# A hybrid decoder block: the third attention group's row maxima with rounded operands and 64-row matmuls, and the last gate evicted without its function

## The chip, the cores and the metric

The kernel runs on one core of a Trainium2 chip. The metric is device time in microseconds (us) of that core. Five engines work side by side: PE (TensorE, matmuls; PEld is its weight loading), DVE (VectorE), ACT (ScalarE), POOL (GpSimd) and SP (SyncE, which here issues nearly all DMAs, in program order, on one queue). Each engine executes its own program in order and waits on semaphores.

## The reference, cut to what matters

The block computes, for 1024 tokens of width 1024, an RMSNorm, one large projection (`z = h @ w_in`), an HGRN2 recurrence over 8 heads, dilated window attention over 3 groups of 8 heads (of 64 channels), a gated merge of both branches and an output projection. The parts that the change touches:

```
q_b = apply_rope(aqkv[:, :, 0], cos, sin);  k_b = apply_rope(aqkv[:, :, 1], cos, sin)
for g, (window, dilation) in enumerate(((128, 1), (512, 4), (2048, 16))):
    s = einsum(q, k) * E ** -0.5, masked;  m = max(s);  p = exp(s - m);  l = sum(p);  o = p @ v
wts = exp(ms - max over groups(ms));  den = sum(wts * l);  num = sum(wts * o)
o_b = num / den * silu(ag)
```

The maximum `m` is subtracted before the exponential and cancels in `num / den`, so it only has to be near the true maximum. In the third group (dilation 16) a sequence of 1024 tokens gives 16 residues of 64 tokens.

## The kernel before, in words

The projection's weights come in chunks of 128 columns (512 KB). Each chunk takes two slots of the program, one for each half of the tokens; in a slot PE runs 24 matmuls of 128x512 (`project`, L682 to L684: rounded high parts and low parts of both operands in three products) into one of two PSUM banks `z_ps[0]` and `z_ps[1]`, and ACT evicts that bank. PE may start the projection of slot s+2 once the bank of slot s is evicted.

First come 8 heads of the recurrence with 6 chunks each. Then come 4 pairs of attention heads with 10 chunks each, that is 20 slots a pair (pairs 0 to 3; pairs 1 and 2 are one hardware loop). After pair 3 comes a tail, in which the last pair's attention is mixed with the first branch products (`branch`, L912 to L914), and then the merge and the output projection.

In a pair, chunks 0 to 5 are q and k of groups 0, 1 and 2 in turn, chunks 6 to 8 the three v, chunk 9 the gate `ag`. For each of the six q and k chunks: ACT evicts it to `zz[0]` (q) or `zz[1]` (k); SP copies `zz` with its 32-row quarters exchanged to `z_swap` (four DMAs of 128 KB, L501); DVE multiplies with cosine and sine (L1638, L1639) and adds (L1643, for group 2 L1603). Groups 0 and 1 are split into rounded high and low parts (`q_two`, `q_sh`, `k_two`, `k_sh`). Group 2 is kept in full f32: DVE's two adds of 64 rows in slot 12 write q to `q_sh[2][0]` and `q_sh[2][1]`, two adds in slot 14 write k to `k_sh[2]`. In these tiles the other 64 rows are zero, but for one row, which holds 1 in `k_sh` and later minus the maximum in `q_sh` (`rows_to_queries`, L441), so that the second product subtracts it.

The row maxima (`maxima`, L797) are matmuls of 128x128 or 128x256 into `pa` (and sometimes `pc`), reduced by DVE (`row_max`, L1524). The eight steps of groups 0 and 1 run behind the projections of slots 8 to 15, two matmul groups each (one per head h); those of group 2 all run behind slot 16. DVE does a slot's reductions in the slot behind. In pairs 1 to 3 PE may write head h of a step only when the same head of the step before is reduced (`mx_taken`, `max_count(u - 1)`; in pair 0 it has `pc` too and waits for `max_count(u - 3)`).

SP's program sets the order of transfers: for each chunk c it first loads the weights of chunk c+2 (L431, when DVE has split chunk c, `w_lo_done`) and then, for c from 1 to 6, issues the four `z_swap` copies of chunk c-1. ACT's eviction of v of group 0 (slot 12, L1196) overwrites `zz[0]` and so waits for DVE's q sums.

In the tail, ACT takes the last exponentials, the high parts of the branch inputs (`branch_hi`, L1244) and of the weights (`branch_w_hi`, L1251), and the logarithm and exponential of the denominators (L1213 to L1216). DVE splits the weights (L1690), and PE's second branch product starts when `w_lo_done` says that they are there. The gate `ag` of a pair is evicted in slots 18 and 19 with ACT's Silu (L1020) to `s_ag`, which is `z_swap`.

Of the kernel before, what the change touches and what calls it, by code (L numbers as in the profile page):

```python
# [28 lines left out]
P = 128  # L29
D_MODEL = 1024  # L30
SEQ = 1024
KT = D_MODEL // P
HEADS = 8
# [4 lines left out]
PAIRS = 4  # L38
EDIM = 64
# [59 lines left out]
def build(nc, d, out):  # L99
# [6 lines left out]
    with ctx:  # L106
# [87 lines left out]
        def place_side(name, g, h):  # L194

            sides[name][g][h] = place(f"{name}{g}{h}", [P, SEQ], f32r if g < 2 else f32)
# [5 lines left out]
        zz = [place(f"zz{s}", [P, SEQ]) for s in range(2)]  # L202
# [12 lines left out]
        m_rows = place("m_rows", [2, GROUPS, SEQ])  # L215
        s_ag, o_b, v_t = z_swap, r_den, zz[0]
# [57 lines left out]
        padded, row_cleared = sem("padded"), sem("row_cleared")  # L274
# [45 lines left out]
        PADS = 19  # L320
# [47 lines left out]
        def _(sp):  # L368
# [64 lines left out]
            def rows_to_queries(i):  # L433

                for g in range(GROUPS):
# [3 lines left out]
                    for h in range(2):  # L439
                        dst = q_sh[g][h][EDIM * (1 - h):EDIM * (1 - h) + 1, :]  # L440
                        sp.dma_start(dst.bitcast(f32) if g < 2 else dst, m_rows[h:h + 1, g, :]).then_inc(rows_in[g], 16)  # L441

            def attention(i, prev, cur):
                for c in range(AT_CHUNKS):
# [42 lines left out]
                    if cur and 1 <= c <= 6:  # L487
# [11 lines left out]
                        for q in range(4):  # L499
                            o = q ^ 1  # L500
                            sp.dma_start(z_swap[32 * q:32 * q + 32, :], zz[(c - 1) % 2][32 * o:32 * o + 32, :]).then_inc(swapped, 16)  # L501
                    if first(i) and c == 4:
# [74 lines left out]
        def _(pool):  # L577
# [28 lines left out]
            def pad_group(g):  # L606

                for h in range(2):
                    other, row = slice(EDIM * (1 - h), EDIM * (2 - h)), slice(EDIM * (1 - h), EDIM * (1 - h) + 1)
                    as_f32 = lambda ap: ap.bitcast(f32) if g < 2 else ap  # L610
                    pad(as_f32(q_sh[g][h][other, :]), 0.0)
# [11 lines left out]

            for i in range(1, PAIRS):
                seen, cleared = value(pool, i * N_UNITS), value(pool, i * 2 - 1)
                pool.wait_ge(const_in, 32)
                pool.wait_ge(st_made, seen)
                nc.gpsimd.memset(q_sh[2][0][EDIM:EDIM + 1, :], 0.0).then_inc(row_cleared, 1)
                pool.wait_ge(row_cleared, cleared)
                nc.gpsimd.memset(q_sh[2][1][0:1, :], 0.0).then_inc(row_cleared, 1)  # L630
# [3 lines left out]
        def _(pe):  # L634
# [138 lines left out]
            def maxima(i, g, m, h):  # L773
# [5 lines left out]
                elif max_bank(i, g, m) is pc:  # L779
                    pe.wait_ge(ob_taken, i * N_SUMS)  # L780
# [4 lines left out]
                if g == 2:  # L785
                    pe.wait_ge(padded, PADS)
                    if not first(i):
                        pe.wait_ge(row_cleared, i * 2)
                    pe.wait_ge(rope_sum, i * 6 + 6)
                else:  # L790
                    pe.wait_ge(qk_lo_done, i * 4 + 2 * g + 2)
                    pe.wait_ge(q_dupped, i * 4 + 2 * g + h + 1)
                for blk, at, before in max_queries(g, m):
                    lo = blk - 1 if before else blk
                    at += 0 if before or g == 2 else P
                    q_side, k_side = (q_two[g][h], k_two[g][h]) if g < 2 else (q_sh[2][h], k_sh[2][h])
                    last = nc.tensor.matmul(max_bank(i, g, m)[:, h, at:at + P * (blk + 1 - lo)], q_side[:, P * blk:P * blk + P],  # L797
                                            k_side[:, P * lo:P * blk + P], start=True, stop=True)
                last.then_inc(mx_made, 1)

            def scores_t(i, u):
# [14 lines left out]
                pe.wait_ge(rope_sum, i * 6)  # L816
                units = unit_keys(g, m)
# [5 lines left out]
                for blk, at, n in units:  # L823
# [4 lines left out]
                    last = nc.tensor.matmul(dst, k_sh[g][h][:, ks], q_sh[g][h][:, qs], start=False, stop=blk == units[-1][0])  # L828
# [20 lines left out]
            def attention(i, prev, cur):  # L849
                for slot in range(2 * AT_CHUNKS):  # L850
# [25 lines left out]
                    if cur:  # L876
                        for g, m in MAX_SLOTS.get(slot, ()):
                            for h in range(2):
                                maxima(i, g, m, h)
# [96 lines left out]
        def _(act):  # L976
# [145 lines left out]
            def attention(i, prev, cur):  # L1122
                for slot in range(2 * AT_CHUNKS):
# [20 lines left out]
                    if cur and 4 <= slot <= 10 and hf == 0:  # L1144
# [6 lines left out]
                        for h in range(2):  # L1151
                            rows = slice(EDIM * h, EDIM * (h + 1))
                            nc.scalar.activation((q_two, k_two)[j % 2][j // 2][h][rows, :], zz[j % 2][rows, :], ACT.Copy).then_inc(qk_hi_done, 1)
# [659 lines left out]
```

## Time and profile before

| | us |
|---|---|
| median of 3 runs | 1509.67 |
| lowest, highest | 1508.07, 1510.61 |
| the profiled execution, its own time | 1508.62 |
| its span, first to last instruction | 1506.5 |
| PE busy | 1488.2 (99%) |
| PE weight loads busy | 1271.6 (84%) |
| DVE busy | 854.9 (57%) |
| ACT busy | 705.1 (47%) |
| granted TensorE clock, mean | 0.999 |

A busy PE is not PE at its peak: matmuls are pipelined, and a matmul's row is longer than its distance to the next one. So the cost of a matmul is read here from start to start.

### The profile page before, as it was taken

To read this page: it belongs to the slowest core of one execution; us is meant where nothing else is said; L and a number is where in the kernel's file an instruction comes from. 1 tells how busy PE (TensorE), PEld (TensorE's weight loads), DVE (VectorE), ACT (ScalarE), POOL (GpSimd) and SP (SyncE) were. 2 spreads that over 40 slices of the span, in tenths; PEclk is the share of its full clock that TensorE was granted. 3 is DMA by queue.
4 is the path that set the end of the run, shared out by engine and by line. 5 is a ranking of instruction groups with operands and counts; after the bars stand their busy time and mean duration, and the time that the engine had idled before them with its cause. 6 is when DMAs were issued, how large, how long until landed. Compare 5 with 4: busy or idle time off the path is not lost. (4 is left out here: it accounts for less than half of the span.)

```text
span 1506.5 us, 21102 instructions
## 1 busy us (share of the span) xinstructions
PE 1488.2 (99%) x7927; PEld 1271.6 (84%) x7927; DVE 854.9 (57%) x1387; ACT 705.1 (47%) x877; POOL 33.3 (2%) x39
## 2 busy tenths in 40 slices
PE   7999999999999999999999999999999999999998
PEld 5888888888888888888888888888888888888987
DVE  6646555473646374667952586358635865644523
ACT  6646565665647474745522434344334435411212
POOL 1000000000000000001400000000000000000000
PEclk9999999999999999999999999999999999999999
DMA  5121111121111211122313212321232134332702
GB/s 217 43 70 57 53 46 69 56 70 56 53 58 56 70 45 66 56 70 71 89 53 87 68 36 79 86 70 33 81 85 70 31 105 135 118 119 100 263 29 84
DMA packets 35520, 116.84 MB, mean 78 GB/s; under 512 B 6200, under 2 KB 6520, under 8 KB 35448
## 3 DMA queue, kind: packets, MB, share of 16 engines
q1 hardware_dynamic: 35456, 115.94, 24.1%
q8 instruction: 46, 0.75, 0.2%
q14 instruction: 18, 0.15, 0.0%
HBM read 83.21 MB, written 20.02 MB: 69 GB/s over the span
## 5 line engine op out<-in xcount | busy, mean ns | idle before, releaser
L682 PE MATMUL z_ps<-h_hi,w_hi 128*128 128x512 f32 x1392 | 551.3, 396 | 0.6 <-ACT zz L1172 0.6
L684 PE MATMUL z_ps<-h_hi,w_lo 128*128 128x512 f32 x1392 | 542.8, 390 | 0.0
L683 PE MATMUL z_ps<-h_lo,w_hi 128*128 128x512 f32 x1392 | 542.2, 390 | 0.0
L684 PEld LDWEIGHTS z_ps<-h_hi,w_lo 128*128 128x128 f32 x1392 | 261.3, 188 | 55.6
L682 PEld LDWEIGHTS z_ps<-h_hi,w_hi 128*128 128x128 f32 x1392 | 261.7, 188 | 52.1 <-issue 1.6
L683 PEld LDWEIGHTS z_ps<-h_lo,w_hi 128*128 128x128 f32 x1392 | 261.8, 188 | 50.4
L1322 DVE TENSOR_TENSOR w_lo<-w_stage,w_hi 128x1024 fp32r<-128x1024 f32 x89 | 109.4, 1230 | 225.7 <-ACT w_hi L1012 225.2
L1020 ACT ACT_TABLE_LOAD x61 | 78.3, 1283 | 77.7 <-PE z_ps L684 77.0
L1120 ACT ACTIVATE pt<-pb 128x512 f32<-128x512 f32 (+1 forms) x80 | 43.4, 543 | 119.5 <-PE pb L828 119.2
L1012 ACT ACTIVATE w_hi<-w_stage 128x1024 fp32r<-128x1024 f32 x89 | 93.8, 1054 | 0.3
L845 PE MATMUL pc<-pt,vb 128*128 128x128 f32 x560 | 77.6, 279 | 1.2 <-ACT pt L1120 1.2
L1379 DVE TENSOR_TENSOR q_lv<-qq,ee 128x512 f32<-128x512 f32 x48 | 33.2, 691 | 74.5 <-ACT ee L1043 74.5
L1043 ACT ACTIVATE ee<-dd 128x1024 f32<-128x1024 f32 x56 | 59.3, 1059 | 26.2 <-DVE dd L1364 25.8
L845 PEld LDWEIGHTS pc<-pt,vb 128*128 128x128 f32 x560 | 69.2, 192 | 1.7 <-ACT pt L1120 1.4
L1172 ACT ACTIVATE zz<-z_ps 128x512 f32<-128x512 f32 x48 | 28.5, 594 | 86.8 <-PE z_ps L684 60.4
L1196 ACT ACTIVATE zz<-z_ps 128x512 f32<-128x512 f32 x24 | 14.4, 598 | 113.9 <-PE pb L894 53.4
L1524 DVE CUSTOM_DVE_ANT_0 pa<-pa,mask_b 128x256 f32<-128x256 f32 (+1 forms) x144 | 48.2, 386 | 12.5 <-issue 7.3
L709 PEld LDWEIGHTS pb<-q_lv,k_lv 128*128 128x128 f32 x384 | 50.2, 191 | 3.7
L1409 DVE COPY_PREDICATED scores<-level_mask,pb 128x512 f32<-128x512 uint8 x48 | 48.3, 1007 | 4.5 <-PE pb L709 3.2
L709 PE MATMUL pb<-q_lv,k_lv 128*128 128x128 f32 x384 | 50.5, 274 | 0.0
L912 PE MATMUL z_ps<-h_hi,w_hi 128*128 128x512 f32 x128 | 50.4, 393 | 0.0
L913 PE MATMUL z_ps<-h_lo,w_hi 128*128 128x512 f32 x128 | 49.8, 389 | 0.0
(257 smaller groups left out, 2202.6 us busy)
## 6 DMA issues: line engine op xcount, KB each, us to landing
w_stage<-w_in SPq DMA_DIRECT2D x88, 512.0 KB, 3.4
z_swap<-zz SPq DMA_DIRECT2D x96, 128.0 KB, 2.3
gate_d<-gate SPq DMA_DIRECT2D x16, 512.0 KB, 4.3
x_in<-x SPq DMA_DIRECT2D x8, 512.0 KB, 7.6
o_a_d<-o_a SPq DMA_DIRECT2D x8, 512.0 KB, 4.7
w_stage<-w_a SPq DMA_DIRECT2D x8, 512.0 KB, 3.8
cos_t<-gate_d SPq DMA_DIRECT2D x8, 512.0 KB, 4.6
sin_t<-gate_d SPq DMA_DIRECT2D x8, 512.0 KB, 3.6
```

Of the source, the lines that this page charges most:

```text
L682: nc.tensor.matmul(z_ps[hf][:], w_hi[s][:, k, :], h_hi[:, k, t], start=k == 0, stop=False)
L683: nc.tensor.matmul(z_ps[hf][:], w_hi[s][:, k, :], h_lo[:, k, t], start=False, stop=False)
L684: last = nc.tensor.matmul(z_ps[hf][:], w_lo[s][:, k, :], h_hi[:, k, t], start=False, stop=k == KT - 1)
L709: last = nc.tensor.matmul(dst[:, P * a:P * a + P], k_side, q_side, start=True, stop=True)
L845: last = nc.tensor.matmul(pc[:, bank, P * ((blk + q) % 4):P * ((blk + q) % 4 + 1)], vb[:, g, blk, EDIM * h:EDIM * h + P], pt[u % 2][:, at ...
L912: nc.tensor.matmul(dst, w_hi[b][:, wk, :], src_hi[:, k, t], start=k == 0, stop=False)
L913: nc.tensor.matmul(dst, w_hi[b][:, wk, :], src_lo[:, k, t], start=False, stop=False)
L1012: nc.scalar.activation(w_hi[s][:], w_stage[s][:], ACT.Copy).then_inc(w_hi_done, 1)
L1020: nc.scalar.activation(dst[:, HALF * hf:HALF * (hf + 1)], z_ps[hf][:], func, **kw).then_inc(z_taken[hf], 1)
L1043: nc.scalar.activation(ee[u % 2][:], dd[u % 2][:], ACT.Exp).then_inc(e_done, 1)
L1322: nc.vector.tensor_tensor(w_lo[s][:], w_stage[s][:], w_hi[s][:].bitcast(f32), ALU.subtract).then_inc(w_lo_done, 1)
L1409: nc.vector.copy_predicated(dst, mask, src).then_inc(lvl_taken, 1)
```

## The change: what it does

Group 2 of every pair:

- In slot 12 DVE makes one add of 128 rows in place in `zz[0]` instead of two of 64 rows. SP copies the two halves by DMA (256 KB each) to `q_sh[2][0]` and `q_sh[2][1]`; it does so between the `z_swap` copies of chunk 4 and the weights of chunk 8 (semaphore `q2_copied`).
- ACT's eviction in slot 12, which overwrites `zz[0]`, waits for these copies. In slot 14 ACT rounds each half into the other tile's other 64 rows (two activations of 64x1024, `q2_rounded`).
- In slot 14 DVE makes a third add, which writes the rounded k of both heads to the new tile `k_hi2` (it lies where `zz[1]` lies).
- The maxima of group 2 are 16 matmuls of 64 contracted rows on rounded operands, the two heads in turn, each head in its own half of the array's rows and its own PSUM bank (`maxima_of_both`). Before they were 16 matmuls of 128 rows in f32, one head after the other.
- GpSimd's clearing of rows of `q_sh[2]` goes, since the DMA copies and the rounding rewrite them.

The last pair's gate is evicted with Copy in slots 18 and 19, and ACT applies Silu in place to the whole 128x1024 tile in the tail's slot 13, behind the high parts of weight chunk 1 of the branches and ahead of the denominators' logarithm.

```diff
                     if cur and 1 <= c <= 6:
...
+                        if c == 5:
...
+                            sp.wait_ge(rope_sum, summed)
+                            if prev:
+                                sp.wait_ge(st_made, scored)
+                            for h in range(2):
+                                rows = slice(EDIM * h, EDIM * (h + 1))
+                                sp.dma_start(q_sh[2][h][rows, :].bitcast(f32), zz[0][rows, :]).then_inc(q2_copied, 16)
...
+            def maxima_of_both(i, m):
+
+                pe.wait_ge(q2_rounded, i * 2 + 2)
+                pe.wait_ge(rope_sum, i * 6 + 6)
...
+                    pe.wait_ge(mx_taken, i * N_MAX + max_count(14 + 2 * m if first(i) else 16))
+                for blk, at, _ in max_queries(2, m):
+                    cols = slice(P * blk, P * blk + P)
+                    for h in range(2):
+                        rows = slice(EDIM * h, EDIM * (h + 1))
+                        last = nc.tensor.matmul(max_bank(i, 2, m)[:, h, at:at + P], q_sh[2][1 - h][rows, cols], k_hi2[rows, cols], start=True, stop=True)
+                        if blk == 4 * m + 3:
+                            last.then_inc(mx_made, 1)
...
+                    if cur and slot == 14:
+
+                        act.wait_ge(q2_copied, i * 32 + 32)
+                        for h in range(2):
+                            rows = slice(EDIM * h, EDIM * (h + 1))
+                            nc.scalar.activation(q_sh[2][1 - h][rows, :], q_sh[2][h][rows, :].bitcast(f32), ACT.Copy).then_inc(q2_rounded, 1)
...
                             if g == 0 and hf == 0:
-                                act.wait_ge(rope_sum, i * 6 + 5)
+                                act.wait_ge(q2_copied, i * 32 + 32)
...
-                            take(n, hf, s_ag, ACT.Silu)
+                            take(n, hf, s_ag, ACT.Copy if isinstance(i, int) and i == PAIRS - 1 else ACT.Silu)
...
+                    if not cur and slot == 13:
+                        for s in range(2):
+                            act.wait_ge(z_taken[s], N_IN)
+                        nc.scalar.activation(s_ag[:], s_ag[:], ACT.Silu)
...
+                    if cur and slot == 12:
+
+                        dve.wait_ge(rope_a, i * 6 + 5)
+                        dve.wait_ge(rope_b, i * 6 + 5)
+                        nc.vector.tensor_tensor(zz[0][:], zz[0][:], z_swap[:], ALU.add).then_inc(rope_sum, 1)
+                    if cur and slot == 14:
...
                         for h in range(2):
                             rows = slice(EDIM * h, EDIM * (h + 1))
-                            dst = (q_sh, k_sh)[j % 2][2][h]
-                            last = nc.vector.tensor_tensor(dst[rows, :], zz[j % 2][rows, :], z_swap[rows, :], ALU.add)
-                        last.then_inc(rope_sum, 1)
+                            last = nc.vector.tensor_tensor(k_sh[2][h][rows, :], zz[1][rows, :], z_swap[rows, :], ALU.add)
+                        last.then_inc(k2_summed, 1)
+                        dve.wait_ge(k2_summed, i + 1)
+                        nc.vector.tensor_tensor(k_hi2[:], zz[1][:], z_swap[:], ALU.add).then_inc(rope_sum, 1)
```

SP's program in the loop of pairs 1 and 2, from the `z_swap` copies of chunk 4 on (`zz_125` is `zz[0]`, `zz_126` is `zz[1]`, `w_stage_52` takes the weights of chunk 8 and `w_stage_53` those of chunk 9). Before:

```order
L501 DMA z_swap<-zz_125 32x1024 x3
L431 ISA [waits w_lo_done,const_in]
L431 DMA w_stage_52<-w_in 128x1024
L301 REGISTER_ALU
L501 DMA z_swap<-zz_126 32x1024 [waits z_taken1,rope_sum,z_taken0,const_in]
L501 DMA z_swap<-zz_126 32x1024 x3
L431 ISA [waits w_lo_done,const_in]
L431 DMA w_stage_53<-w_in 128x1024
```

And now:

```order
L507 DMA z_swap<-zz_125 32x1024 x3
L305 ISA
L521 DMA q_sh_135<-zz_125 64x1024 [waits st_made,rope_sum,const_in]
L521 DMA q_sh_136<-zz_125 64x1024
L435 ISA [waits w_lo_done,const_in]
L435 DMA w_stage_52<-w_in 128x1024
L507 DMA z_swap<-zz_126 32x1024 [waits z_taken1,rope_sum,z_taken0,const_in]
L507 DMA z_swap<-zz_126 32x1024 x3
L435 ISA [waits w_lo_done,const_in]
L435 DMA w_stage_53<-w_in 128x1024
```

Both the q copies and the `z_swap` copies of chunk 5 wait for the same DVE sum (`rope_sum`, slot 12). Before, the weights of chunk 8 were issued ahead of that wait and the swap came first behind it; now two q copies and the weights stand between the sum and the swap.

ACT's program in the tail, from the last exponentials to the weights of the second branch product (`w_hi_54`). Before:

```order
L1120 ACTIVATE pt_131<-pb 128x512
L1244 ACTIVATE ob_hi<-sin_t 128x1024
L1244 ACTIVATE ob_hi<-zz_125 128x1024
L1251 ACTIVATE w_hi_55<-w_stage_53 128x512
L1213 ACT_TABLE_LOAD
L1213 ACTIVATE r_den<-acc_132 64x1024
L1214 ACTIVATE r_den<-acc_133 64x1024
L1216 ACT_TABLE_LOAD
L1216 ACTIVATE r_den<-r_den 128x1024
L1251 ACTIVATE w_hi_54<-w_stage_52 128x1024
```

And now:

```order
L1145 ACTIVATE pt_131<-pb 128x512
L1279 ACTIVATE ob_hi<-sin_t 128x1024
L1279 ACTIVATE ob_hi<-zz_125 128x1024
L1286 ACTIVATE w_hi_55<-w_stage_53 128x512
L1245 ACT_TABLE_LOAD
L1245 ACTIVATE z_swap<-z_swap 128x1024
L1248 ACT_TABLE_LOAD
L1248 ACTIVATE r_den<-acc_132 64x1024
L1249 ACTIVATE r_den<-acc_133 64x1024
L1251 ACT_TABLE_LOAD
L1251 ACTIVATE r_den<-r_den 128x1024
L1286 ACTIVATE w_hi_54<-w_stage_52 128x1024
```

A table load and the Silu of 128x1024 now stand ahead of the logarithms and of `w_hi_54`.

## Rows read from the trace of the kernel before

**Rows 1.** The page, busy time of each engine, share of the span and instructions

```profile
PE 1488.2 (99%) x7927; PEld 1271.6 (84%) x7927; DVE 854.9 (57%) x1387; ACT 705.1 (47%) x877; POOL 33.3 (2%) x39
```

**Rows 2.** Timeline, PE, pair 1 slot 16: start us, us, operation, count, idle before

```profile
923.79 1.95 PE L797 MATMUL pa<-k_sh,q_sh 128*128 128x128 f32 x16
925.57 1.95 PE L797 MATMUL pc<-k_sh,q_sh 128*128 128x128 f32 x16
927.36 1.04 PE L894 MATMUL pb<-ident,zz 128*128 128x128 f32 x8
```

**Rows 3.** Timeline, weight loads of rounded operands, one unit of scores in the tail

```profile
1263.68 0.19 PEld L828 LDWEIGHTS pb<-q_sh,k_sh 128*128 128x128 f32 x1
1263.80 0.19 PEld L827 LDWEIGHTS pb<-q_two,k_two 128*128 128x128 f32 x1
```

**Rows 4.** Timeline, DVE, pair 1, slots 12 to 14

```profile
898.86 2.47 DVE L1603 TENSOR_TENSOR q_sh<-zz,z_swap 64x1024 f32<-64x1024 f32 x2
...
905.60 1.98 DVE L1638 TENSOR_TENSOR zz<-zz,cos_t 128x1024 f32<-128x1024 f32 x1 [1.73 <-DMA z_swap<-zz]
...
910.66 0.43 DVE L1524 CUSTOM_DVE_ANT_0 pa<-pa,mask_b 128x256 f32<-128x256 f32 x1
...
911.01 2.45 DVE L1603 TENSOR_TENSOR k_sh<-zz,z_swap 64x1024 f32<-64x1024 f32 x2
913.49 1.23 DVE L1322 TENSOR_TENSOR w_lo<-w_stage,w_hi 128x1024 fp32r<-128x1024 f32 x1
```

**Rows 5.** Timeline, SP's DMA issues, the same stretch

```profile
901.41 2.41 SPq L501 DMA_DIRECT2D z_swap<-zz  x4
904.07 0.38 SPq L431 DMA_DIRECT2D w_stage<-w_in  x1
```

**Rows 6.** The page, DMA issues: count, KB each, median us from issue to landing

```profile
w_stage<-w_in SPq DMA_DIRECT2D x88, 512.0 KB, 3.4
z_swap<-zz SPq DMA_DIRECT2D x96, 128.0 KB, 2.3
```

**Rows 7.** Timeline, PE, pair 1: starts of slot 14, its maxima, slot 16's start

```profile
905.34 0.39 PE L682 MATMUL z_ps<-h_hi,w_hi 128*128 128x512 f32 x1
...
910.79 0.92 PE L797 MATMUL pa<-k_two,q_two 128*128 128x128 f32 x4
...
918.34 0.39 PE L682 MATMUL z_ps<-h_hi,w_hi 128*128 128x512 f32 x1
```

**Rows 8.** Timeline, ACT, pair 1: evictions of slots 12 and 14

```profile
901.36 0.60 ACT L1196 ACTIVATE zz<-z_ps 128x512 f32<-128x512 f32 x1 [8.19 <-DVE q_sh L1603]
...
912.62 0.60 ACT L1196 ACTIVATE zz<-z_ps 128x512 f32<-128x512 f32 x1 [5.99 <-PE pb L894]
```

**Rows 9.** Timeline, ACT, the start of the tail

```profile
1248.04 0.60 ACT L1020 ACTIVATE z_swap<-z_ps 128x512 f32<-128x512 f32 x1 [3.42 <-PE z_ps L684]
1248.66 1.28 ACT L1120 ACT_TABLE_LOAD   x1
1249.95 0.60 ACT L1120 ACTIVATE pt<-pb 128x512 f32<-128x512 f32 x1
```

**Rows 10.** Timeline, PE, the same place

```profile
1249.13 0.28 PE L828 MATMUL pb<-q_sh,k_sh 128*128 128x256 f32 x1
1250.60 1.16 PE L845 MATMUL pc<-pt,vb 128*128 128x128 f32 x8 [1.19 <-ACT pt L1120]
```

**Rows 11.** Timeline, the tail's slot 13: ACT

```profile
1286.72 1.28 ACT L1213 ACT_TABLE_LOAD   x1
...
1292.44 1.04 ACT L1251 ACTIVATE w_hi<-w_stage 128x1024 fp32r<-128x1024 f32 x1
```

**Rows 12.** Timeline, DVE and then PE, behind it

```profile
1293.54 1.22 DVE L1690 TENSOR_TENSOR w_lo<-w_stage,w_hi 128x1024 fp32r<-128x1024 f32 x1
...
1294.81 0.19 PEld L912 LDWEIGHTS z_ps<-h_hi,w_hi 128*128 128x128 f32 x1 [0.20 <-DVE w_lo L1690]
1294.88 0.44 PE L912 MATMUL z_ps<-h_hi,w_hi 128*128 128x512 f32 x1
```

More of the change, by code:

```diff
@@ L201, in build @@
             place_side(name, g, h)
-        zz = [place(f"zz{s}", [P, SEQ]) for s in range(2)]
+        zz = [place("zz0", [P, SEQ])]
+        zz1_at = top[0]
+        zz.append(place("zz1", [P, SEQ]))
         z_swap = place("z_swap", [P, SEQ])
@@ L622, in _ @@
             assert pads[0] == PADS
[L624 to L630, printed above, removed]
         @block.tensor
@@ L784, in maxima @@
                     pe.wait_ge(mx_taken, i * N_MAX)
[L785 to L792, printed above, removed]
+                pe.wait_ge(qk_lo_done, i * 4 + 2 * g + 2)
+                pe.wait_ge(q_dupped, i * 4 + 2 * g + h + 1)
                 for blk, at, before in max_queries(g, m):
                     lo = blk - 1 if before else blk
[L795 to L798, printed above, removed]
+                    at += 0 if before else P
+                    last = nc.tensor.matmul(max_bank(i, g, m)[:, h, at:at + P * (blk + 1 - lo)], q_two[g][h][:, P * blk:P * blk + P],
+                                            k_two[g][h][:, P * lo:P * blk + P], start=True, stop=True)
                 last.then_inc(mx_made, 1)
+            def maxima_of_both(i, m):
+                pe.wait_ge(q2_rounded, i * 2 + 2)
+                pe.wait_ge(rope_sum, i * 6 + 6)
+                if max_bank(i, 2, m) is pc and not first(i):
+                    pe.wait_ge(ob_taken, i * N_SUMS)
+                else:
+                    pe.wait_ge(mx_taken, i * N_MAX + max_count(14 + 2 * m if first(i) else 16))
[6 more added lines that the diff above has]
+                            last.then_inc(mx_made, 1)
             def scores_t(i, u):
@@ L827, in scores_t @@
                         nc.tensor.matmul(dst, k_two[g][h][:, ks], q_two[g][h][:, qs], start=False, stop=False)
-                    last = nc.tensor.matmul(dst, k_sh[g][h][:, ks], q_sh[g][h][:, qs], start=False, stop=blk == units[-1][0])
+                    q_side = q_sh[g][h][:, qs] if g < 2 else q_sh[g][h][:, qs].bitcast(f32)
+                    last = nc.tensor.matmul(dst, k_sh[g][h][:, ks], q_side, start=False, stop=blk == units[-1][0])
                 last.then_inc(st_made, 1)
@@ L877, in attention @@
                         for g, m in MAX_SLOTS.get(slot, ()):
-                            for h in range(2):
-                                maxima(i, g, m, h)
+                            if g == 2:
+                                maxima_of_both(i, m)
+                            else:
+                                for h in range(2):
+                                    maxima(i, g, m, h)
                     if cur and slot == 17:
```

31 lines of the change are left out of this document (20 added, 11 removed).

## The prediction, made before the changed kernel ran

> **What bounds the kernel now.** I read the busy times first: PE is busy 99% of the span and no other engine over 57% [rows 1]. So the end is set by PE's program, and only two things count: PE work that goes, and time in which PE waits. I then read PE's timeline where the changed matmuls stand, and for each new wait the timeline of the engine that PE would wait for, to see how near PE already is to it. There are two such places: the maxima of slot 14, which run late behind DVE's reductions, and the tail's slot 13, where PE's weight load already waits for DVE's split. All sums are made against the profiled execution (1508.62 us; its span is 1506.5, and 2.1 lie around it, untouched). It is 1.05 under the median 1509.67; the difference that I find is put on the median.
>
> **Slot 16, the matmuls that go.** In pair 1 the group-2 maxima begin at 923.79 and the transposes behind them at 927.36, so 16 f32 products, 32 instructions in the trace, take 3.57 us or 0.111 each, start to start [rows 2]. All four pairs have these 32. After, there are 16 instructions of 128 columns on rounded operands. The nearest rows: weight loads of rounded operands follow each other at 0.12 us (1263.68, 1263.80) [rows 3], and the f32 instructions, a load each, at 0.111. If each of the 16 needs a weight load of its own at 0.111 in a row, they take 1.78 and save 1.79 a pair. The other end: the two heads lie in different halves of the array's rows, so a pair of them might go side by side, 8 x 0.111 = 0.89, saving 2.68. On the dear side, entering and leaving the half-row form may empty the pipeline: an f32 instruction's row is 1.95 - 15 x 0.111 = 0.28 long [rows 2], 0.17 more than its distance, so twice 0.17 or 0.34 a pair, saving 1.45. No 64-row matmul stands in this trace. I take 1.79, the value of the nearest row: 4 x 1.79 = **-7.2 us**. The Trainium skill, TensorEngine Tiling (Array Packing), section Tiling Modes, says that changing the tiling mode drains the engine; by that the saving would be 1.45 a pair and the whole result 1.4 higher. This trace can't show it.
>
> **Slot 12, the copies.** DVE's q sum is one instruction of 1.23 instead of 2.47, so in pair 1 it ends at about 900.1 instead of 901.33 [rows 4]. SP then issues two copies; at 0.6 each, as for the four swaps in 2.41 [rows 5], the second goes out at about 900.8. A 128 KB swap lands in 2.3 us, 512 KB of weights in 3.4 [rows 6], so 256 KB land within that, by 904.2 at the latest. ACT's eviction of slot 12 (0.60) [rows 8] then ends by 904.8; PE wants the bank at 905.34 [rows 7]. That wait costs nothing, with at least 0.5 us of cover; each us beyond would be a us of PE. ACT's two roundings in slot 14 (2.1 together; a 64-row activation costs as much as a 128-row one) fall into the 5.99 us for which it idles there [rows 8]. GpSimd's memsets go for nothing: no one waits for them.
>
> **Slots 13 and 14, what is late next.** Behind the q sum SP used to issue the four swaps of chunk 5 at once: 901.41 to 903.82 [rows 5], and DVE, which waited 1.73 us for them, began at 905.60 [rows 4], 1.78 behind the last issue. Now SP issues two copies (1.2), the weights of chunk 8 (0.4) and then the swaps (2.41), from about 900.2. If only the issues count, DVE begins at 900.2 + 4.0 + 1.78 = 906.0: 0.4 late. If the transfers queue: 384 KB more land 1.1 us later [rows 6], about 350 KB a us; the first piece lands at 900.2 + 2.3, the other 1.4 MB take 4.0, so 906.5 to 906.6, 1.0 late. If the whole of the weights' landing (3.4) went ahead of a swap's (2.3), it would be 907.5, 1.9 late. I take 0.9. This goes one for one to PE: DVE's last reduction of slot 13 is over at about 911.1 [rows 4], and PE's maxima of slot 14, from 910.79, already take 0.92 instead of the usual 0.62 [rows 7] because head 1 must wait for it. So the stall grows by all that DVE is late, in pairs 1 and 2, and in pair 3, whose maxima of slot 14 stand equally close. Pair 0 has a second bank and waits for an older reduction. 3 x 0.9 = **+2.7 us**, with ends at 1.2 and 5.7.
>
> DVE's third add of k costs 1.23 and a short wait. With 0.9 of lateness the split of chunk 8's weights ends at 913.49 + 1.23 + 0.9 + 1.3 = 916.9 [rows 4], where PE wants them at 918.34 [rows 7], itself then 0.9 later. Hidden; without that cover it would be 1.3 a pair.
>
> **The tail, first place.** ACT evicts the gate until 1248.64, loads Exp's table (1.28) and starts the first exponential at 1249.95 [rows 9]; PE idles 1.19 for it [rows 10]. With Copy the table stays as it was. The exponential then waits only for the scores: the last matmul of the first unit ends about 0.1 behind the eviction, PE goes on at about 1249.4. That gives **-1.2 us**; it can't give more than 1.35. The table load of slot 18 goes too, but ACT idles there.
>
> **The tail, second place.** A table load (1.28) and a Silu of 128x1024 (1.06, as the 1.04 of the same shape [rows 11]) come ahead of the logarithms. ACT works without a gap from the last exponential to `w_hi` at 1292.44 [rows 11], so `w_hi` comes 2.34 later, DVE's split, which follows it by 0.06, too, and PE's weight load waited 0.20 for that split already [rows 12]. So PE waits the whole **+2.3 us**. Its bounds: 0 if something else moved ahead, 2.4 by the rows. The denominators' product, also 2.34 late, is needed only after 48 matmuls, 11 us on. The Trainium skill, ScalarE: Activation LUTs, section What ACT_TABLE_LOAD costs, gives 1.28 us for the load and about 1.38 for a drain, 2.66 per switch. The load agrees, but the activation starts 0.01 after it (1248.66 + 1.28 against 1249.95), so I add no drain; with it this term would be 3.7.
>
> **Sum:** -7.2 + 2.7 - 1.2 + 2.3 = -3.4 on the profiled execution, so 1505.3 there and **1506.3 us** as a median.
>
> **Rivals.**
> 1. The two heads' matmuls run side by side: 0.89 a pair for slot 16, 3.6 less than the forecast, 1502.7. For: heads in turn, different rows of the array, different banks. Against: each instruction still brings 128 columns of weights, and every row here spaces those by 0.11 or more. The same page of the Trainium skill says under Key Properties that tiles run weight loads and matmuls in parallel.
> 2. Slower: the swaps of slot 13 come much later, since 1 MB stands ahead of them in one queue. DVE's lateness enters three times; from 2.1 us each (900.2 to 907.7 at DVE's start) it eats the gain. At 2.5 the sum is -7.2 + 7.5 + 1.1 = +1.4, 1511.1; at 3.2 it is +3.5, and the split of chunk 8 becomes late too. For: the queue is one, DVE already waits at this spot. Against: even all transfers in a row account for 1.9.
> 3. The change doesn't bring what it says in slot 16: alternating between halves makes each matmul wait for the one before, 0.28 instead of 0.111 apart, so 16 take 4.5 instead of 3.57. The sum is 4 x 0.9 + 2.7 + 1.1 = +7.4, 1517.
> 4. Both new stalls are covered after all (swaps hardly late, Silu beside other work): -7.2 + 1.2 - 1.2 = -7.2, 1502.5.
>
> **Chances.** Forecast 0.42 (its own range 1504.5 to 1508.5), rival 1 0.32, rival 2 0.14, rival 3 0.05, rival 4 0.07. Differences below 0.2%, 3.0 us, count as none, about what a measurement of this kernel can tell. The forecast lies close to that bound: over half of its chance, 0.23, is faster, 0.19 the same. Rivals 1 and 4 are faster, rival 2 half same and half slower, rival 3 slower. Faster 0.62, same 0.26, slower 0.12. The range 1502.0 to 1511.0 leaves out what is beyond rival 2's middle and the extremes of rival 1.
>
> **What would show it.** Right: in slot 16 the start of the maxima to that of the transposes near 1.8 us (0.9 for rival 1, over 3.5 for rival 3); DVE's wait for the swap in slot 13 longer and the maxima of slot 14 stretched from 0.9 to about 1.8 in pairs 1 to 3 (over 3 for rival 2); the idle 1.19 in front of the first weighted sum of the tail gone; in the tail's slot 13 a new wait of PE of about 2.3 for the split weights. Wrong: a PE wait of over 0.5 for ACT's slot 12 eviction at slot 14, or for chunk 8's weights at slot 16.

## The result: 0.85% slower, where 0.2% faster was forecast

| | before | after |
|---|---|---|
| median, us (4 executions each, same chip) | 1509.76 | 1522.80 |
| ratio, 95% interval | | 1.0085 [1.0073, 1.0097] |
| profiled execution, us | 1508.62 | 1522.04 |
| its span, us | 1506.5 | 1519.9 |
| granted TensorE clock, mean | 0.999 | 0.994 |

The time is outside the range 1502 to 1511. Of all executions below one was slow (of `b1_half_f32_late_silu`: 1856.2 us at a granted clock of 0.753); that kernel's ratio leaves it out, its median counts it. Every difference is taken from PE's landmarks in the two profiled executions, which lie 13.4 us apart.

PE's busy time is the one of [rows 1], almost to the digit, though PE does less work: part of it runs at a lower clock. The page's busy row, then the view of what PE waited for:

```profile
PE 1488.1 (98%) x7863; PEld 1267.3 (83%) x7863; DVE 853.9 (56%) x1387; ACT 713.4 (47%) x885; POOL 25.8 (2%) x31
```

```profile
engine line waited for: us in total, times, longest us
PE pa L801 <- DVE m_all L1559: 10.6, 4, 3.6
...
PE z_ps L937 <- DVE w_lo L1730: 2.1, 1, 2.1
PE z_ps L695 <- DVE w_lo L1357: 1.4, 1, 1.4
...
PE z_ps L695 <- ACT zz L1227: 0.8, 1, 0.8
```

The first line is slot 14 in pairs 1 to 3: PE wants to write the maxima of slot 14, and DVE has not reduced those of slot 13. The second is the tail's slot 13. The third and the fourth stand in pair 0. The tail's wait for the first exponential [rows 10] is gone.

**Slot 16** is shorter than forecast. PE's timeline of pair 1, to hold against [rows 2]:

```profile
929.74 0.66 PE L817 MATMUL pa<-k_hi,q_sh 64*128 64x128 f32 x8
930.24 0.61 PE L817 MATMUL pc<-k_hi,q_sh 64*128 64x128 f32 x8
930.78 1.10 PE L919 MATMUL pb<-ident,zz 128*128 128x128 f32 x8
```

Start to start 1.04 us instead of 3.57, on average 0.065 for each of the 16 matmuls. From slot 16's maxima to PE's transpose of `m_all` behind slot 17's projection it is 7.45 instead of 9.93 (7.46 in pair 0): 4 x 2.48 = 9.9 us gained.

**Slots 12 to 14** are where the time went. SP, DVE and PE of pair 1, to hold against [rows 5], [rows 4] and [rows 7]:

```profile
900.34 1.15 SPq L521 DMA_DIRECT2D q_sh<-zz  x2
901.75 0.40 SPq L435 DMA_DIRECT2D w_stage<-w_in  x1
902.32 2.80 SPq L507 DMA_DIRECT2D z_swap<-zz  x4
905.37 0.38 SPq L435 DMA_DIRECT2D w_stage<-w_in  x1
```

```profile
909.93 1.95 DVE L1678 TENSOR_TENSOR zz<-zz,cos_t 128x1024 f32<-128x1024 f32 x1 [7.24 <-DMA z_swap<-zz]
...
914.01 0.30 DVE L1559 CUSTOM_DVE_ANT_0 pa<-pa,mask_b 128x128 f32<-128x128 f32 x1 [0.34 <-DVE z_swap L1679]
```

```profile
905.04 0.62 PE L801 MATMUL pa<-k_two,q_two 128*128 128x128 f32 x4
...
914.82 1.43 PE L801 MATMUL pa<-k_two,q_two 128*128 128x128 f32 x4 [3.57 <-DVE m_all L1559]
916.05 1.91 PE L919 MATMUL pb<-ident,zz 128*128 128x128 f32 x8
```

The copies take SP's queue at 900.34. The swap's last issue is over at 905.12 instead of 903.82, and then 4.8 us pass until DVE begins instead of 1.78. DVE starts 4.33 us later than before, its reductions follow at 914.01, and PE idles 3.57. The eight transposes behind the wait last 1.91 where such eight last 1.04 [rows 2]. The stretches of time say why (us; busy time of PE, PEld, DVE, ACT, POOL; granted clock; DMA share; GB/s), for pair 1 and then for pair 3, the last line over exactly the time in which its clock was low:

```profile
910.00:914.00 4.00, 1.25 (x6) 0.70 (x4) 3.67 (x2) 1.07 (x2) 0.00 (x0) 1.00 0.01 3
914.00:918.00 4.00, 3.04 (x13) 2.85 (x14) 3.94 (x11) 0.01 (x1) 0.00 (x0) 0.68 0.02 4
...
1220.00:1224.00 4.00, 0.82 (x3) 0.69 (x4) 3.87 (x11) 0.00 (x0) 0.00 (x0) 0.83 0.00 0
1222.61:1229.43 6.82, 6.25 (x20) 5.44 (x21) 6.77 (x19) 2.96 (x4) 0.00 (x0) 0.50 0.15 37
```

Behind the wait the granted clock falls to 0.50 (1.2 GHz), for 3.4 us in pairs 1 and 2 (915.41 to 918.82 and 1069.01 to 1072.42) and for 6.8 in pair 3. From the maxima of slot 13 to those of slot 16 pairs 1, 2 and 3 take 24.70, 24.08 and 25.81 us instead of 18.91, 18.93 and 18.71: 18.0 us lost.

**The tail.** To the first weighted sum 1.22 us are gained, as forecast. In its slot 13 PE waits as forecast:

```profile
1306.65 0.50 PE L937 MATMUL z_ps<-h_hi,w_hi 128*128 128x512 f32 x1 [2.08 <-DVE w_lo L1730]
...
1308.35 0.63 PE L937 MATMUL z_ps<-h_hi,w_hi 128*128 128x512 f32 x1
1309.63 0.63 PE L937 MATMUL z_ps<-h_hi,w_hi 128*128 128x512 f32 x1
```

The last two rows are three matmuls and 1.28 us apart, 0.43 each instead of 0.23: the clock is slow here too, 0.58 from 1308 to 1312, and that costs another 1.7.

### The profile page after: what moved, and what is told of

It is laid out like the page before. It is cut to its first block and busy times, and to the rows that moved or that the text cites. A ratio compares the mean times of both kernels' runs of the same rounds, so it can differ in the third digit from the quotient of the medians.

```text
span 1519.9 us, 20978 instructions
## 1 busy us (share of the span) xinstructions
PE 1488.1 (98%) x7863; PEld 1267.3 (83%) x7863; DVE 853.9 (56%) x1387; ACT 713.4 (47%) x885; POOL 25.8 (2%) x31
## 5 line engine op out<-in xcount | busy, mean ns | idle before, releaser
L697 PE MATMUL z_ps<-h_hi,w_lo 128*128 128x512 f32 x1392 | 543.3, 390 | 0.0
L696 PE MATMUL z_ps<-h_lo,w_hi 128*128 128x512 f32 x1392 | 543.2, 390 | 0.0
L1678 DVE TENSOR_TENSOR zz<-zz,cos_t 128x1024 f32<-128x1024 f32 x24 | 41.7, 1738 | 33.9 <-DMA z_swap<-zz 29.7
L1559 DVE CUSTOM_DVE_ANT_0 pa<-pa,mask_b 128x256 f32<-128x256 f32 (+1 forms) x144 | 48.2, 384 | 13.4 <-issue 12.4
L939 PE MATMUL z_ps<-h_hi,w_lo 128*128 128x512 f32 x128 | 50.6, 395 | 0.0
```

The lines of the kernel that those rows point to most:

```text
L696: nc.tensor.matmul(z_ps[hf][:], w_hi[s][:, k, :], h_lo[:, k, t], start=False, stop=False)
L697: last = nc.tensor.matmul(z_ps[hf][:], w_lo[s][:, k, :], h_hi[:, k, t], start=False, stop=k == KT - 1)
L939: last = nc.tensor.matmul(dst, w_lo[b][:, wk, :], src_hi[:, k, t], start=False, stop=k == kt - 1)
```

## The experiments

The question was which part of the new order makes the swap late (the two copies' issues, their data, the load that now stands between), how much of the loss is the clock, and why the 64-row matmuls take so little time. The runs came in three groups, each beside runs of the kernel before on the same chip (medians 1509.34, 1509.53, 1509.69).

### Each half of the change alone

`e2_pairs_only`: the pairs' part, with the last gate evicted as before.

```
-   take(n, hf, s_ag, ACT.Copy if isinstance(i, int) and i == PAIRS - 1 else ACT.Silu)
+   take(n, hf, s_ag, ACT.Silu)                 # and no Silu in the tail's slot 13
```

> The changed kernel with the tail as before: the rounded 64-row maxima with their copies alone. Theory: the pairs' part makes nearly all of the loss: slot 16 saves 2.5 us in each pair, the waits of slots 13 and 14 with the slow clock behind them cost 5 to 7 us in each of pairs 1 to 3 and 2.9 in pair 0. Net +10.5 us, about 1520.3. Rival (tail and pairs share the loss): below +7 us.

Measured 1518.81, ratio 1.0067 [1.0051, 1.0082], where 1520.3 was expected; PE waits for `m_all` in slot 14, three times 3.2 to 3.5 us. Most of the loss, 9.5 of 13.0 us by the medians, is in the pairs.

`e1_tail_only`: the kernel before with only the gate's raw eviction and the Silu in the tail's slot 13.

> The kernel before with the change's tail part alone (last gate evicted raw, Silu ahead of the logarithms). Theory: the two parts add up. The 1.2 us wait for the first exponential goes; PE waits 2.2 us for the split weights in slot 13, and its granted clock falls behind that wait, which costs 1.7 us more, as in the changed kernel. Net +2.7 us, about 1512.4. Rival (the clock falls only because PE had lost time before, in the pairs): +1.0 us, 1510.8, with the granted clock 1.00 around 1295 to 1300 us. Rival (the Silu is free): -1.2 us.

Measured 1511.30, 1.0013 [1.0004, 1.0022], so +2.0 us with an interval of 0.6 to 3.3, which holds the theory's +2.7 and the first rival's +1.0. The 1.2 us wait goes, the 2.1 us wait for `w_lo` comes. In the profiled execution the clock stays up behind it:

```profile
1292.00:1296.00 4.00, 1.92 (x9) 1.28 (x8) 1.97 (x2) 2.00 (x2) 0.00 (x0) 1.00 0.06 24
1296.00:1300.00 4.00, 4.00 (x19) 3.28 (x18) 2.84 (x3) 1.06 (x2) 0.00 (x0) 1.00 0.77 262
```

The same wait of 2.1 us stands in eight of the profiled executions. Behind it the granted clock fell to 0.50 for 3.4 us in four (the changed kernel, `h1`, `h2` and `g1` below) and stayed at 1.00 in four (`e1`, `e4`, `e5`, `w1`). The rival's reason, time lost before in the pairs, does not decide it: in `h2` no wait in the pairs is over 0.6 us and the clock falls, while in `e5` and `w1` the pairs lose more and it does not. The view of `h2`, behind its wait in the tail:

```profile
1290.07:1293.49 3.42, 3.42 (x10) 2.65 (x9) 2.44 (x2) 0.89 (x1) 0.00 (x0) 0.50 0.85 296
```

What decides between them is open.

### What makes the swap late: a table of two by two

`h1_small_copies`, the changed kernel with nearly empty copies:

```
-   sp.dma_start(q_sh[2][h][rows, :].bitcast(f32), zz[0][rows, :])
+   sp.dma_start(q_sh[2][h][rows, 0:64].bitcast(f32), zz[0][rows, 0:64])
```

> The changed kernel, but each of the two q copies moves 64 of 1024 columns (16 KB instead of 256 KB); so the third group's scores and maxima are computed from mostly zero queries, and all instructions stay. Theory (the bytes ahead of the swaps and their slow rate make them late): with 0.5 MB gone, the swaps of slot 13 land at least 2 us earlier relative to their issue, PE's waits in slot 14 shrink from 3.6 us to under 1.5 us each, and the slow clock behind them goes; total 1510 to 1514. Rival (the time in which SP issues two copies and the weights, 1.7 us, and the order make them late): the waits stay at 3 us or more, total above 1519.

Measured 1512.80, 1.0026 [1.0016, 1.0036]. The time is within what was expected, the wait isn't: it should have fallen under 1.5, and it is 2.51, 1.57 and 1.40 in pairs 1, 2 and 3, the first two with a slow clock behind them. The copies' data are not the main thing.

`e4_weights_first`, the changed kernel with one move in SP's program:

```
     chunk 5:  swap of chunk 4
-              copies of q                       (wait for DVE's q sum)
     chunk 6:  weights of chunk 8
+              copies of q
               swap of chunk 5
```

> The changed kernel with one order changed in SP's queue: the two copies of q are issued behind the load of weights that followed them, so that copies and swaps stand next to each other and no load between. Theory (what makes the swap late is the 512 KB of weights plus the slow copies in one queue ahead of it): the swaps go out about 0.5 to 1 us earlier and only 256 KB stand ahead of them, DVE begins its third rope at about 907.5 instead of 909.9, PE's wait in slot 14 of pairs 1 to 3 falls from 3.6 to about 1.5 and with it the slower clock: 3 x 2 to 3 us less, 1514 to 1517. Rival (the copies alone delay it, the load is quick): the wait stays above 3 and the time within 2 us of 1522.8.

Measured 1506.55, 0.9981 [0.9971, 0.9990]: 16 us below the changed kernel and 3 below the kernel before. The waits in slot 14 are 0.8 us instead of 3.6, and the clock stays at 1.00. More than the theory gave it. SP's timeline shows why the load costs nothing in this place:

```profile
881.94 0.34 SPq L435 DMA_DIRECT2D w_stage<-w_in  x1
900.31 1.15 SPq L508 DMA_DIRECT2D q_sh<-zz  x2
901.63 2.83 SPq L521 DMA_DIRECT2D z_swap<-zz  x4
904.72 0.37 SPq L435 DMA_DIRECT2D w_stage<-w_in  x1
```

What the load waits for is done long before the q sum: it goes out at 881.94, and in the kernel before at 881.78. In the changed kernel it stands in program order behind the copies, which wait for that sum, and is held back for 20 us, into the one place where DVE waits for the queue.

`h2_small_copies_weights_first`: both edits.

> The kernel with the weights first and, beside that, copies of 64 of q's 1024 columns only: the same two issues, 16 KB in place of 256 KB each... so the maxima and scores of the third group are wrong in the other columns. Theory (with no load and almost no copy ahead of it the swap costs DVE only the two issues): DVE begins its third rope of pair 1 at about 906.2 instead of 906.9 with whole copies and 909.9 in the changed kernel, PE's waits in slot 14 shrink from 0.8 to about 0.2 each: 1.5 to 2 us under the run with weights first, 1504.5 to 1505. Rival (the load matters and the copies do not): DVE still at 906.9, no change.

Measured 1503.15, 0.9956 [0.9940, 0.9973]. No wait in slot 14 over 0.2. A little better than the 1504.5 to 1505 expected: counted from SP's first issue DVE begins after 5.56 us, where 5.9 were expected.

`e5_swap_first`: the copies behind the swap of chunk 5, with the weights ahead of it.

> The changed kernel with the copies of q issued behind the swap of chunk 5 instead of ahead of it. Theory (copies and swap share one way, and whichever comes second is late for its reader): DVE begins its rope on time (905.6 in pair 1), PE's waits for the reductions in slot 14 are gone, but ACT can evict slot 12 only when the copies have landed, at about 907.5, and PE waits for that bank at the start of slot 14, 2.5 to 3 us in each of four pairs, with a slower clock behind it: 1514 to 1519. Rival (the copies are hidden there): no wait at slot 14, 1503 to 1504, the best of all orders.

Measured 1517.15, 1.0055 [1.0038, 1.0072]. As the theory had it: no wait for `m_all` in slot 14, and instead

```profile
PE z_ps L695 <- ACT zz L1227: 11.3, 4, 3.4
```

Whichever of the two goes second, someone waits, and in this order ACT's eviction of slot 12.

In one table, from SP's first issue of pair 1 to DVE's first product, and the way from slot 13's to slot 16's maxima, summed over pairs 1 to 3:

| | first issue | DVE begins | between | slots 13 to 16, sum |
|---|---|---|---|---|
| before (swap only) | 901.41 | 905.60 | 4.19 | 56.6 |
| small copies, load elsewhere (h2) | 899.41 | 904.97 | 5.56 | 57.6 |
| whole copies, load elsewhere (e4) | 900.31 | 906.93 | 6.62 | 60.6 |
| small copies, load between (h1) | 898.10 | 906.49 | 8.39 | 66.9 |
| whole copies, load between (after) | 900.34 | 909.93 | 9.59 | 74.6 |

The effects add up: two more issues 1.37, the copies' data 1.1 to 1.2, the load 2.8 to 3.0. That is 5.4 together; the shorter q sum gives 1.07 back, and DVE is 4.33 late. More than half of it is the load. In pair 1 the swap's copies land 2.3 us after their issue (median) before and with small copies alone (h2), 3.4 with whole copies (e4), 4.1 with the load (h1) and 4.7 with both. The load's place in the queue costs SP 0.6 (from the first copy's issue to the swap's it is 1.95 in h1 and 1.32 in h2); why it costs 2.8 to 3.0 in all is not shown.

### How much of it is the clock

`w1_keep_running`: the changed kernel, with work in PE's wait.

```
+   if cur and prev and slot == 14:
+       pe.wait_ge(ob_taken, i * N_SUMS)
+       for t in range(16):
+           nc.tensor.matmul(pc[:, 0, :], h_hi[:, 0, 0:P], h_hi[:, 0, 0:HALF], start=True, stop=True)
```

> The changed kernel with 16 matmuls more (rounded, 128 x 512, into a bank that is overwritten behind them) in slot 14 of pairs 1 to 3, ahead of the third group's maxima, in the time in which PE would wait for DVE. It tells the wait from the slower clock behind it. Theory (of 5.2 to 7.1 us that a pair loses there 3.6 are the wait and the rest the lower granted clock that follows it): the wait is filled by 16 x 0.23 = 3.6 us of work, the clock stays at 1.00 and the maxima begin when they did: 1.6 to 3.5 us a pair come back, 4 to 6 in all, 1517 to 1519. Rival (the surplus is the reductions and the transposes waiting for DVE step by step, not the clock): no change from 1522.8.

Measured 1516.76, 1.0056 [1.0041, 1.0070]: 6 us less than the changed kernel by the medians (4.4 by the ratios, since the two ran beside different runs of the kernel before), by doing more. PE's rows of pair 1, and the stretch behind the filling:

```profile
912.97 3.79 PE L901 MATMUL pc<-h_hi 128*128 128x512 f32 x16
916.94 1.13 PE L801 MATMUL pa<-k_two,q_two 128*128 128x128 f32 x4 [0.19 <-DVE m_all L1563]
917.91 1.04 PE L923 MATMUL pb<-ident,zz 128*128 128x128 f32 x8
...
916.00:920.00 4.00, 3.67 (x22) 2.80 (x21) 3.82 (x11) 1.00 (x2) 0.00 (x0) 1.00 0.02 4
```

The transposes are back at 1.04 and the clock at 1.00. Slots 13 to 16 take 23.35, 22.69 and 23.13 us, 12.6 above before in sum. So of the 18.0 us lost there 12.6 are DVE's lateness (4.2 a pair, against 4.33 at DVE), and 5.4 the slower clock behind the wait. That is a lower end for the clock: in pairs 2 and 3 PE has nothing left to wait for behind the filling, which may itself be a little longer than the wait was. The profiled execution also has no slow clock in the tail, where the changed kernel's lost 1.7; that is not the filling's work.

### Why the 64-row matmuls take so little time

`g1_heads_in_order`: four matmuls of head 0, then four of head 1.

```
-   for blk, at, _ in max_queries(2, m):
-       for h in range(2):
+   for h in range(2):
+       for blk, at, _ in max_queries(2, m):
```

> The changed kernel with one edit: the 8 half-row matmuls of a bank go out as four of head 0 and then four of head 1, no longer in turn. Theory (a matmul of one half runs beside its neighbour's of the other half, 0.065 us each in turn, and two of the same half can't): 16 matmuls take about 1.8 us instead of 1.04, so 0.75 a pair, 3 us in all: 1525.8 against 1522.8. Rival (they are fast because rounded 64-row matmuls are short in themselves, whichever half they are in): still 1.04, and the time of the changed kernel.

Measured 1523.82, 1.0097 [1.0082, 1.0111], the changed kernel's ratio within both intervals; the theory's 1525.8 is within this run's as well, so the time alone decides nothing. What it expected of slot 16 falls: 16 matmuls take 1.10 us, not 1.8.

```profile
931.17 0.67 PE L817 MATMUL pa<-k_hi,q_sh 64*128 64x128 f32 x8
931.67 0.67 PE L817 MATMUL pc<-k_hi,q_sh 64*128 64x128 f32 x8
932.27 1.10 PE L919 MATMUL pb<-ident,zz 128*128 128x128 f32 x8
```

But the rival's reason, short in themselves, does not follow. Counts of the matmuls in flight, in stretches of 0.03 or 0.04 us around the first starts, tell more (length, PE busy, matmuls in flight, clock, DMA share, GB/s): the kernel before, the changed kernel, then this run.

```profile
923.78:923.81 0.03, 0.02 (x1) 1.00 0.00 0
923.88:923.91 0.03, 0.03 (x2) 1.00 0.00 0
923.99:924.02 0.03, 0.03 (x3) 1.00 0.00 0
...
929.72:929.75 0.03, 0.01 (x2) 1.00 0.00 0
929.88:929.91 0.03, 0.03 (x4) 1.00 0.00 0
930.00:930.03 0.03, 0.03 (x6) 1.00 0.00 0
...
931.16:931.20 0.04, 0.03 (x2) 1.00 0.00 0
931.32:931.36 0.04, 0.04 (x4) 1.00 0.00 0
931.44:931.48 0.04, 0.04 (x6) 1.00 0.00 0
```

Before, one matmul starts every 0.11 us. In the changed kernel two start together, 3 or 4 ns apart, and the pairs follow each other at 0.11 (929.902, 930.016, 930.125). In this run it is the same with 13 ns between the two. They can't be two of the same half: in each bank only the fourth matmul of each head signals DVE, and by the trace's semaphore records the two that signal are the seventh and eighth to start (931.559 and 931.573); in the order of the program head 0's would be the fourth. All four pairs of heads show this. So the two heads run side by side, in two halves of the array's rows, and PE takes up head 1's matmuls beside head 0's even where they stand behind them in its program. Within one half the distance stays 0.11, as with 128 rows. The theory had the reason right, and that the heads must come in turn wrong.

`f1_half_rows_f32`: the kernel before with the 64-row form alone, in f32. No copies, no rounding, no third add; GpSimd's clearing of rows goes too, as in the changed kernel.

```
+   last = nc.tensor.matmul(max_bank(i, 2, m)[:, h, at:at + P], q_sh[2][h][rows, cols],
+                           k_sh[2][h][rows, cols], start=True, stop=True)
```

> The kernel before, with only the form of the group-2 maxima changed: 64 contracted rows, the heads in turn, in f32, straight from the tiles that are there; no rounding, no copies, no third add, no clearing of rows. Theory (two heads side by side in the two halves of the array, two instructions per f32 product): slot 16's maxima take 16 x 0.11 = 1.8 us instead of 3.57, a gain of 1.8 us a pair with no new wait: -7.1 us, 1502.6. Rival (only rounded operands go side by side, or the load of weights is the bound for f32): no gain in slot 16, 1509.7, or a loss if the halves drain between instructions.

Measured 1502.51, 0.9960 [0.9946, 0.9973]: all that was expected, by an edit of a few lines:

```profile
922.24 1.16 PE L806 MATMUL pa<-k_sh,q_sh 64*128 64x128 f32 x16
923.23 1.06 PE L806 MATMUL pc<-k_sh,q_sh 64*128 64x128 f32 x16
924.22 1.09 PE L906 MATMUL pb<-ident,zz 128*128 128x128 f32 x8
```

32 f32 instructions take 1.98 us, on average 0.062 each, against 0.111 with 128 rows [rows 2]. Here too they start two at a time, 7 ns apart, and the next two 0.11 us later (922.449 and 922.456, 922.561 and 922.568). So running the two heads side by side nearly halves the time, in f32 as well as rounded; rounding halves the number of instructions. In slot 16 the form gives 1.59 of 2.53 us a pair, the rounding 0.94, and the rounding is what needs the copies and the third add. No run has 64-row matmuls of one half alone; that they would be no faster than those of 128 rows is read from their distance within a half.

### The tail repaired, and the best kernels

`a1_after_late_silu`: the changed kernel, the Silu behind `w_hi` of the tail's slot 14.

```
-   if not cur and slot == 13:    (wait for both banks; Silu of s_ag)
+   (at the end of slot 14's entry in the tail:)
+   nc.scalar.activation(s_ag[:], s_ag[:], ACT.Silu).then_inc(den_done, 1)
```

> The changed kernel with its last Silu moved behind w_hi of the tail's slot 14, nothing else. Theory (the Silu's place costs a wait of 2.1 us, and in the changed kernel also a slower clock behind it, 1.7): 1522.8 - 3.9 = 1518.9. Rival (only the wait, the clock is the chip's mood in that one execution): 1522.8 - 2.2 = 1520.6.

Measured 1519.86, 1.0063 [1.0046, 1.0080], between the two expectations; the wait for `w_lo` is gone. Against the changed kernel, which ran in another group, it can't tell 2.2 from 3.9, and a slow clock behind such a wait comes in some executions only.

`c1_weights_first_late_silu`: both repairs.

> The changed kernel with both repairs: the copies of q behind the load of weights in SP's queue (as in the run weights first, 1506.6), and the last Silu behind w_hi of the tail's slot 14. Theory (the tail's wait of 2.1 us for w_lo comes from the Silu's place alone, and nothing else stands there): 1506.6 - 2.2 = 1504.4, still 2 us behind the f32 half rows without copies, since DVE is late by more than a us in pairs 1 to 3. Rival (the late Silu puts off the logarithms and the division, which PE then waits for): 1506 or more.

Measured 1504.02, 0.9963 [0.9949, 0.9977], as the theory had it.

`b1_half_f32_late_silu`: the f32 half rows, and the last gate evicted raw with the late Silu.

> The kernel before with the two heads' third-group maxima in half of the rows (64), heads in turn, on the f32 sums that are there anyway (no copies of q, no rounding, no third add), and with the last pair's gate evicted raw, its Silu moved behind the split of the last weights (w_hi of the tail's slot 14), where ACT idles. Theory (what the changed kernel lost hangs on the copies and on the Silu's place, not on the half-row maxima or on the raw gate): -7 us for the maxima as in the run with f32 half rows alone, -1.2 for the wait at the start of the tail, and no new wait for w_lo in the tail's slot 13: 1509.5 - 8.2 = 1501.3. Rival (the late Silu delays the logarithms and the division that end the tail): the maxima alone, 1502.5, or worse by up to 1.

Measured 1502.80, 0.9957 [0.9944, 0.9969]. In the profile the 1.2 us wait at the tail's start is gone and no wait comes for it; the median does not show the gain over f32 half rows alone. The profiled executions differ already at pair 0 by 1.84 us (slot 16's maxima at 774.23 against 772.39), partly a longer first load of `x_in` (8.8 us waited, against 7.9), and that covers it. This kernel, the f32 half rows alone and the changed kernel with both repairs (0.9957, 0.9960, 0.9963) all beat the kernel before and can't be told apart.

## Why the prediction was wrong, step by step

| step | forecast | measured |
|---|---|---|
| slot 16, 16 matmuls, four pairs | -7.2 | -9.9 |
| slots 13 and 14, pairs 1 to 3 | +2.7 | +18.0 (12.6 late, 5.4 clock) |
| pair 0 | 0 | +2.9 |
| tail, the first exponential | -1.2 | -1.2 |
| tail, the wait for `w_lo` | +2.3 | +2.2, and 1.7 clock |
| sum | -3.4 | +13.7 (13.4 by the profiled executions) |

**The step that failed** is the transfers' time in "slots 13 and 14". The mechanism was named, and the place; "This goes one for one to PE" held too (4.2 a pair for 4.33 at DVE). The size of DVE's lateness was put at 0.9 and was 4.33, more than double the upper end of 1.9. Rival 2, at 0.14, was this mechanism with 2.5 to 3.2. Three things were wrong in the step. First, "If only the issues count" and "If the transfers queue" were set against each other, and the runs show that the costs add: 1.37 for two more issues, 1.1 to 1.2 for the copies' data, 2.8 to 3.0 for the load, less 1.07 for the shorter q sum. Second, the upper end let the swap land 3.4 + 2.3 = 5.7 us after the load's issue; DVE began 8.18 behind it (901.75 to 909.93). Third, the value of 0.9 rested on "384 KB more land 1.1 us later, about 350 KB a us", a difference between landing times of two kinds of transfers: a swap within SBUF and a load from HBM. They don't move at one rate. Rows of before that stood in the same trace would have said so (stretches of 2 us, the last two columns are DMA share and GB/s; the first is swap alone, the last load alone):

```profile
902.00:904.00 2.00, 2.00 (x11) 1.65 (x10) 1.87 (x9) 0.00 (x0) 0.00 (x0) 1.00 0.72 160
904.00:906.00 2.00, 2.00 (x12) 1.75 (x11) 0.40 (x1) 0.93 (x2) 0.00 (x0) 1.00 0.90 201
906.00:908.00 2.00, 2.00 (x10) 1.66 (x9) 2.00 (x2) 0.62 (x1) 0.00 (x0) 1.00 0.40 164
```

Divided by the share, the engines move 222 GB/s of swap (160 / 0.72) and 410 of load (164 / 0.40). Both are rough, since in a stretch this short the share can exceed 1 (1.10 in the changed kernel from 902 to 904). The changed kernel between 902 and 910 has the engines nearly full:

```profile
902.00:906.00 4.00, 4.00 (x21) 3.37 (x20) 0.69 (x5) 1.09 (x2) 0.00 (x0) 1.00 0.98 255
906.00:910.00 4.00, 4.00 (x20) 3.27 (x19) 0.07 (x1) 2.00 (x2) 0.00 (x0) 1.00 0.91 235
```

That is 1.96 MB in 8 us, the load at 905.37 included, which shares the engines with the swap's end. With 222 for the 0.9 MB of copies and swap behind the first piece and 410 for the 0.5 MB of weights the forecast's own rule would have given 4.1 + 1.3 = 5.4 us instead of its 4.0, and DVE's start at 907.9, 2.3 late: near rival 2, and still 2.0 short. Nor do its terms fit the runs: it charges the copies' 0.5 MB 2.4 us, where they cost 1.1 to 1.2, and the load 1.3, where it costs 2.8 to 3.0. So the right rates would have moved the forecast the right way, but they don't explain the loss; what makes the load that dear is open. A part may be the load issued at 905.37; no run takes that one away. The Trainium skill, DMA: Bandwidth & Descriptors, section Where 436 GB/s comes from, says that transfers within SBUF are bound by the fabric's 435 GB/s; here copies and swaps alone reached 225 GB/s at a DMA share of 0.97 (weights first, 902 to 904), about half. They are of 32 or 64 rows each; no run has one of 128.

**What was missing altogether** is the clock. No term and no rival had it: at least 5.4 us in the pairs and 1.7 in the tail, 7 of the 13.4. The trace before shows no PE wait of this size in mid-program, and its granted clock is 1.00 around both places, so it could not be read there. The runs do price it: each of the 14 PE waits of 2.87 to 3.86 us in the pairs, in five kernels, was followed by 3.4 or 6.8 us at 0.50. Shorter waits, from 1.57 to 2.56 us, were followed by a slow clock in some cases and not in others.

**Slot 16**: rival 1 was right, in its number (0.89 a pair; 1.04 measured) and in its reason, the two heads side by side. The forecast took the distance of full-row weight loads [rows 3] for each of the 16 instructions; it holds within a half, and the halves run beside each other. A cost at the change of form is there, smaller than the 0.34 a pair of the dear end: the first maximum starts 0.32 behind the last projection's matmul where it was 0.23, the second two 0.16 behind the first two where 0.11 is usual, and the first transpose 0.20 behind the last maximum's start where it was 0.11, in sum 0.24. That it is an emptying of the pipeline is not shown.

**Slot 12, the copies** "costs nothing": right for pairs 1 to 3, where ACT evicts at 904.79 and PE doesn't wait. The copies landed in 3.6 us (median), where "by 904.2 at the latest" had 3.4. Pair 0 waits 0.8 for this eviction. **The split of chunk 8** "Hidden": right for pairs 1 to 3 and wrong for pair 0, where PE is not itself late and waits 1.43, by the load that was held back. Both were named as what would prove the prediction wrong; pair 0, with 2.25 us of waits and 0.7 behind them, makes 2.9 of the 13.4 us.

**The tail**: both terms right, to 0.1 us. The Silu follows its table load by 0.01 us, as [rows 9] had it for the exponential, so the drain of about 1.38 that the Trainium skill, ScalarE: Activation LUTs, section What ACT_TABLE_LOAD costs, adds isn't there:

```profile
1296.22 1.28 ACT L1245 ACT_TABLE_LOAD   x1
1297.51 1.06 ACT L1245 ACTIVATE z_swap<-z_swap 128x1024 f32<-128x1024 f32 x1
```

## What to carry to other kernels

An instruction that waits, put into a queue that works in program order, holds back all behind it: for each DMA look up when it was issued before, and what it meets at its new time. Add the costs of issues, of data and of a load in between; here none of them hid another. Take a transfer's rate from stretches in which its own kind runs alone, bytes over share, not from the landing time of another kind, and don't expect the rate to give a load's whole cost. Give a long PE wait a price above its length. When a run's time comes out the same, that does not choose between two reasons: here the starts of single matmuls did. And try the cheapest part of a change by itself: here the 64-row form on the data that were there gave as much as all of it repaired.

## What the runs showed of the hardware that was not expected

- Matmuls that contract 64 rows in different halves of the array's rows start two at a time, 3 to 13 ns apart, and the next two 0.11 us later, the distance of single ones with 128 rows: 0.062 us each on average in f32 and 0.065 rounded, against 0.111. With four of one head issued ahead of four of the other they still run side by side (0.069): the fourth of head 0 starts behind the first three of head 1.
- DMA within SBUF, in copies of 32 or 64 rows, moves 202 to 232 GB/s by its share (160 / 0.72; 225 / 0.97; 182 / 0.90 in `e5` from 906 to 908), loads of weights about 410 (164 / 0.40).
- A load of 512 KB issued ahead of four copies within SBUF made their reader 2.8 to 3.0 us later, 512 KB of copies in the same place 1.1 to 1.2.
- Behind waits of 2.9 to 3.9 us the granted clock fell to 0.50 for 3.4 or 6.8 us, behind waits of 2.1 us in four executions of eight; with the changed kernel's three gaps of 3.3 to 3.6 us filled by matmuls of no use it stayed at 1.00, and the kernel was 4 to 6 us faster.
